# Gated-recurrence keys multiplied by their bound in place, and the diagonal level's products issued with levels 3 and 4

## The chip, the cores and the metric

One core of a Trainium2 chip runs one program. The metric is the device time of one execution in microseconds (us). Engines are named as in the profile: PE (TensorE matmul), PEld (its weight loads), DVE (VectorE), ACT (ScalarE), POOL (GpSimd), SP (SyncE, which here only issues DMAs).

## The reference

Four blocks run one after the other on 256 tokens of width 2048: a gated convolution, the gated recurrence (HGRN2), sliding-window attention, a SwiGLU feed-forward. The change is in the recurrence. Per direction and head (16 heads of 128):

```python
def forget(a, lb):
    log_f = jnp.logaddexp(jnp.log(lb), jnp.log1p(-lb) + jax.nn.log_sigmoid(a))
    key = (1.0 - lb) * jax.nn.sigmoid(-a)
    return heads(log_f), heads(key)
...
        b = jnp.cumsum(fb, axis=2)
...
        decay = jnp.exp(jnp.where(lower_tri, diff, -jnp.inf))
        scores = jnp.einsum("bhtk,bhsk,bhtsk->bhts", qb, kb, decay)
        o_intra = jnp.einsum("bhts,bhsv->bhtv", scores, vb)
```

`lb` is the lower bound of the forget gate. Both directions are added, normalised per head, gated and projected.

## The kernel before

**Weights as the clock of the program.** All weight matrices stream through four slots in chunks of 256 x 512 numbers, 656 of them. For each chunk SP loads `raw`, ACT rounds it to `w_hi` (L889), DVE subtracts to get `w_lo` (L1273; POOL does it in some stretches), and PE issues 12 matmuls of 128 x 512 (L625, L626, L627: w_hi by h_hi, w_lo by h_hi, w_hi by h_lo). ACT may round chunk n once PE has used chunk n-4, DVE waits for ACT, and PE waits for DVE. All other work is hung on this stream: `Hooks` is a table from a tick (the chunk's place in its phase, from 0) to the steps that an engine issues, in program order, right behind its own instruction for that chunk. On PE the steps of tick 8 stand behind the matmuls of chunk 8.

**The recurrence.** The input projection of the recurrence has four iterations of 32 chunks, one for each group j of four heads. The work on group j is issued during the next iteration, and for the last group in the phase that follows (the gate projection). These four stretches, 100 us each from about 470 us on, are called **passes 1 to 4** here (j = 0 to 3), and ticks are counted from 0 to 31 within a pass. Scores are not taken from one product, because the decay between two tokens is a difference of running sums. They are taken in levels: level 1 is the product of the two halves of 128 tokens, levels 2 to 8 are pairs of neighbouring blocks of 64, 32, 16, 8, 4, 2, 1 tokens, and level 0 is the diagonal (a token with itself, no decay). In a pass:

- POOL moves three transposed tiles in blocks of 32 partitions (L503): `kf`, `kb` (the gate inputs of both directions), `qT`, 16 copies each. It is set going by DVE's transposes at tick 28 of the pass before (`quarters`).
- ACT: `gates(0)` at tick 1, `gates(1)` at tick 6 (sigmoids of kf and kb, both signs, behind POOL's moves), `ln_f` for the two directions at 6 and 7, `ln_k` at 8 and 9, `take(0)` at 11, the exponentials of level 1 at 12 and 13, then at 11+2s the exponentials of level s and at 15, 17, 20 `take` of levels 1, 2, 3 (copies out of PSUM).
- DVE: `diagonal` at 6, `scan_f` at 8 and `scan_b` at 9 (running sums), `keys` at 10 and 11, `diffs(2)` at 12, and from 13 on `weigh(s)` at 11+2s and `diffs(s+1)` at 12+2s; `take` of levels 4 to 8 from 21 on.
- PE: level 0 at tick 8, level 1 at 13, level 2 at 14, levels 3 and 4 at 18, 5 and 6 at 22, 7 and 8 at 26, then the products with the values at 26 and 28.

`diagonal` (L1438 on) forms kf x bound + kb x bound into a slot of `E`; `ln_k` takes the logarithm of key x bound, with the bound as ACT's scale, one head at a time, since each head has its own column of bounds. It waits for `diagonal`, since it overwrites the keys. Steps tell each other by counting semaphores: `g_G` (DVE's operands are ready), `g_mm` (PE's level is in PSUM), `g_S` (it has been taken from there). `g_mm` and `g_S` are incremented in the order in which levels are issued.

Of the kernel before, what the change touches and what calls it, by code (L numbers as in the profile page):

```python
# [30 lines left out]
ACT = mybir.ActivationFunctionType  # L31
ALU = mybir.AluOpType
# [4 lines left out]
S = 256  # L37
# [12 lines left out]
HPG = GC // P  # L50
# [114 lines left out]
def build(nc, t, out):  # L165
    ph = phases()
    ctx = ExitStack()
    with ctx:
# [13 lines left out]
        fg = sb(ctx, "fg", [P, TB, GC])  # L182
        ident = sb(ctx, "ident", [P, P])
        feat = sb(ctx, "feat", [P, KT, ROWS])
        eps = sb(ctx, "eps", [P, 2])
# [23 lines left out]
        lbj = sb(mix, "lbj", [P, 2, 2, HPG])  # L209
# [24 lines left out]
        qT = sb(hs, "qT", [P, HPG, S])  # L234
        kf = sb(hs, "kf", [P, HPG, S])
        kb = sb(hs, "kb", [P, HPG, S])
        Bc = sb(hs, "Bc", [P, HPG, S])
        Xc = sb(hs, "Xc", [P, HPG, S])
        E = sb(hs, "E", [P, 2, 2, HPG, S])
        ST = sb(hs, "ST", [P, 2, HPG, 2, P])  # L240
        SB = sb(hs, "SB", [P, HPG, 2, QUARTER])
# [2 lines left out]
        ssh = sb(hs, "ssh", [P, 3, 2 * HPG])  # L244
        powers = sb(hs, "powers", [P, 2 * HPG])
        gate_rows = (aftok, abtok, qtok, sz)
        lf_back = qtok[:, :, :].rearrange("p a (b c) -> p (a b) c", c=S)
        hs.close()

# [26 lines left out]
        T = ctx.enter_context(nc.psum_tensor("T", [P, 4, 512], F32))  # L276
# [2 lines left out]

        def operands(s):  # L280

            b = (s - 1) % 4 if s else 1
            return (E_more if b >= 2 else E)[:, b % 2, :, :, :]

        def gate_banks(k):
            return T01 if k % 2 else T23
# [76 lines left out]
        def flat(ap):  # L363
            return ap.rearrange("p a b -> p (a b)")
# [205 lines left out]
        def _(pe):  # L570
# [138 lines left out]
            at = Hooks().put(4, lambda: v_turn(3))  # L709
# [11 lines left out]
            def level(j, s):  # L721

                pe.wait_ge(g_G, 9 * j + s + 1)
                if s == 0:
                    pe.wait_ge(g_M, 3 * j + 3)
                if s >= 2:
                    pe.wait_ge(g_K, 7 * j + s - 1)
                    pe.wait_ge(g_S, 9 * j + s - 1)
                e = operands(s)
                for h in range(HPG):  # L730
                    for b in range(2):
                        if s == 1:
                            last = nc.tensor.matmul(T[:, h // 2, (h % 2) * S + b * P:(h % 2) * S + b * P + P],  # L733
                                                    e[:, 0, h, b * P:(b + 1) * P], e[:, 1, h, (1 - b) * P:(2 - b) * P],
                                                    start=True, stop=True)
                            continue
                        n = HB if s == 2 else QUARTER
                        for i in range(P // n):
                            at = b * P + i * n
                            to = b * P + (i ^ 1) * n if s in (2, 3) else at  # L740
                            g, q = (e[:, 1, h, at:at + n], qT[:, h, to:to + n]) if s == 0 else (e[:, 0, h, at:at + n], e[:, 1, h, to:to + n])
                            last = nc.tensor.matmul(T[i * n:(i + 1) * n, 2 + s % 2, (2 * h + b) * n:(2 * h + b + 1) * n],  # L742
                                                    g, q, start=True, stop=True)
                last.then_inc(g_mm, 1)

# [10 lines left out]

            def av_across(j):
                pe.wait_ge(g_raw, 4 * j + 4)
                pe.wait_ge(g_S, 9 * j + 2)
                av_products(True)  # L760

            def av(j):
# [2 lines left out]

            def process(j):

                at = Hooks().put(8, lambda: level(j, 0))
                for s in range(1, 9):
                    at.put(13 if s == 1 else 10 + 4 * (s // 2 + s % 2) if s > 2 else 14, lambda s=s: level(j, s))  # L770
                return at.put(26, lambda: av_across(j)).put(28, lambda: av(j))
# [98 lines left out]
        def _(act):  # L870
# [199 lines left out]
            def ln_k(j, d):  # L1070

                act.wait_ge(g_G, 9 * j + 1)
                k = (kf, kb)[d]
                for h in range(HPG):
                    last = A(k[:, h, :], k[:, h, :], ACT.Ln, scale=lbj[:, d, 1, h:h + 1], bias=eps[:, 1:2])
                last.then_inc(g_act, 1)

            def cross_keys(j):

                act.wait_ge(g_D, 15 * j + 1)  # L1080
                for h in range(HPG):
                    A(E[:, 0, 0, h, 0:P], kf[:, h, 0:P], ACT.Exp, bias=Bc[:, h, P - 1:P])
                    A(E[:, 0, 0, h, P:S], kb[:, h, P:S], ACT.Exp, bias=back[:, 1, h:h + 1])

            def cross_queries(j):
                for h in range(HPG):
                    A(E[:, 0, 1, h, 0:P], Xc[:, h, 0:P], ACT.Exp, scale=-1.0, bias=Xc[:, h, P:P + 1])
                    last = A(E[:, 0, 1, h, P:S], Bc[:, h, P:S], ACT.Exp, bias=back[:, 0, h:h + 1])
                last.then_inc(g_E, 1)
# [6 lines left out]

            def take(j, s):

                act.wait_ge(g_mm, 9 * j + s + 1)
                if s == 0:  # L1100
                    A(SB[:, :, :, :].rearrange("p a b c -> p (a b c)"), T[:, 2, 0:S], ACT.Copy).then_inc(g_S, 1)
                    return
                if s == 1:
                    if not is_first(j):
                        act.wait_ge(g_av, j)
                    A(ST[:, 0, :, :, :].rearrange("p a b c -> p (a b c)"), flat(T01), ACT.Copy).then_inc(g_S, 1)
                    return
                c = LEVELS[s - 2]
                ps = T[:, 2 + s % 2, 0:2 * HPG * c].rearrange("p (a c) -> p a c", c=c)
                for i in range(P // c):  # L1110
                    r, o = slice(i * c, (i + 1) * c), (i ^ 1) * c
                    last = A(ST[r, 1, :, :, o:o + c].rearrange("p a b c -> p (a b) c"), ps[r, :, :], ACT.Copy)
                last.then_inc(g_S, 1)
# [15 lines left out]
            def process(j):  # L1129
                at = Hooks().put(1, lambda: gates(j, 0)).put(6, lambda: gates(j, 1))  # L1130
                for d in range(2):
                    at.put(6 + d, lambda d=d: ln_f(j, d)).put(8 + d, lambda d=d: ln_k(j, d))
                at.put(11, lambda: take(j, 0)).put(12, lambda: cross_keys(j)).put(13, lambda: cross_queries(j))
                for s in range(1, 9):
                    if s > 1:
                        at.put(14 if s == 2 else 11 + 2 * s, lambda s=s: exp(j, s))
                    if s < ACT_TAKES:
                        at.put((15, 17, 20)[s - 1], lambda s=s: take(j, s))
                return at.put(29, lambda: blocks(j)).put(31, lambda: o_out(j))
# [112 lines left out]
        def _(dve):  # L1252
# [185 lines left out]
            def diagonal(j):  # L1438

                dve.wait_ge(g_lb, j + 1)  # L1440
                dve.wait_ge(g_act, 6 * j + 2)
                for h in range(HPG):
                    V.tensor_scalar(E[:, 1, 1, h, :], kf[:, h, :], lbj[:, 0, 1, h:h + 1], None, ALU.mult)
                settle()
                for h in range(HPG):
                    last = STT(out=E[:, 1, 1, h, :], in0=kb[:, h, :], scalar=lbj[:, 1, 1, h:h + 1],
                               in1=E[:, 1, 1, h, :], op0=ALU.mult, op1=ALU.add)
                last.then_inc(g_G, 1)

            def scan_f(j):  # L1450

# [38 lines left out]
            def diffs(j, s):  # L1490

                e = operands(s)
                dve.wait_ge(g_mm, 9 * j + max(1, s - 3))
                c = width(s)
                rf, rb = bounds(c)
                fr, bl = halves(Bc[:, :, :], c)[1], halves(Xc[:, :, :], c)[0]
                kl, kr = halves(kf[:, :, :], c)[0], halves(kb[:, :, :], c)[1]
                gl, gr = halves(e[:, 0, :, :], c)
                ql, qr = halves(e[:, 1, :, :], c)
                TT(ql, rb, bl, ALU.subtract)  # L1500
                TT(qr, fr, rf, ALU.subtract).then_inc(g_D, 1)
                TT(gl, rf, kl, ALU.add)
                TT(gr, kr, rb, ALU.subtract).then_inc(g_D, 1)
# [9 lines left out]
            def take(j, s):  # L1513

                settle()
                if s == ACT_TAKES:
                    dve.wait_ge(g_S, 9 * j + s)
                dve.wait_ge(g_mm, 9 * j + s + 1)
                V.memset(none[:, :], 0.0)
                V.copy_predicated(SB[:, :, :, :].rearrange("p a b c -> p (a b) c"),  # L1520
                                  lmask[:, s - ACT_TAKES, :].unsqueeze(1).to_broadcast([P, 8, QUARTER]),
                                  T[:, 2 + s % 2, 0:S].rearrange("p (a c) -> p a c", c=QUARTER)).then_inc(g_S, 1)
# [300 lines left out]
```

## Time and profile before

| | |
|---|---|
| median of 3 runs | 1899.8 us (1899.09 to 1900.17) |
| the profiled execution's own time | 1899.58 us |
| its span | 1897.3 us |
| PE busy | 1891.8 us |
| PEld busy | 1560.9 us |
| DVE busy | 1286.2 us |
| ACT busy | 1057.8 us |
| POOL busy | 614.4 us |
| TensorE clock granted | full in all 40 slices |

How to read it: the span is what the profile covers; 2.3 us of the execution lie around it. Matmuls are recorded as overlapping (a 128 x 512 matmul shows 0.39 us, but the next one starts 0.227 us after it), so PE's busy time says little about its waits: they are read from the distance between the starts of two matmuls. A float32 matmul of the levels leaves two records, so the 32 matmuls of level 0 count as x64 in the trace.

### The profile page before, as it was taken

The page shows a single profiled execution, that of the slowest core. Times are in us where ns is not written, and L with a number is a line of the kernel's source. Part 1 is how long each engine was busy: PE and PEld are TensorE (multiplying, and loading weights), DVE is VectorE, ACT ScalarE, POOL GpSimd, SP SyncE. Part 2 cuts the span into 40 slices and gives each one's busy share as a digit, 9 for nine tenths or more (in the row PEclk, how much of TensorE's full clock was granted, in tenths as well). Part 3 has the DMA queues.
Part 4 walks back from the last instruction along what each step waited for, and adds up shares of the span by engine and source line. Part 5 has one row for each costly group of instructions (what it writes and reads, how often), then busy time and mean ns, then how long its engine had stood idle before and what let it go on. Part 6 is the DMA issues. An engine that isn't in the chain of part 4 may idle for free.

```text
span 1897.3 us, 28818 instructions
## 1 busy us (share of the span) xinstructions
PE 1891.8 (100%) x10864; PEld 1560.9 (82%) x10864; DVE 1286.2 (68%) x1869; ACT 1057.8 (56%) x1402; POOL 614.4 (32%) x641
## 2 busy tenths in 40 slices
PE   9999999999999999999999999999999999999999
PEld 8888878888887888788888888888888888888887
DVE  5899967555888888887668876555555555544443
ACT  7444466456868787875465755444444444443432
POOL 1899852306051423302418641122222222210000
PEclk9999999999999999999999999999999999999999
DMA  9666555666555565555565455666666666655554
GB/s 326 193 190 186 178 171 194 189 195 182 168 176 167 151 185 167 167 161 184 189 190 150 154 174 171 206 191 196 188 191 196 193 194 191 195 193 195 192 195 159
DMA packets 183598, 352.62 MB, mean 186 GB/s; under 512 B 11840, under 2 KB 12352, under 8 KB 183488
## 3 DMA queue, kind: packets, MB, share of 16 engines
q1 hardware_dynamic: 183344, 351.12, 60.1%
q8 instruction: 72, 1.18, 0.3%
q14 instruction: 38, 0.31, 0.0%
q10 hardware_dynamic: 144, 0.01, 0.0%
HBM read 348.99 MB, written 2.10 MB: 185 GB/s over the span
## 4 chain that ended last, share of the span: by engine, by line
PE 88%; DVE 4%; POOL 4%; issue 2%; ACT 2%; DVEq 1%; POOLq 0%; ACTq 0%
PE acc L625 28%; PE acc L627 28%; PE acc L626 28%; POOL kb L503 2%; POOL kf L503 1%; DVE w_lo L1273 1%; PE T L576 1%; DVEq L1259 1%; PE T L742 1%; PE acc L592 1%; PE T L843 0%; ACT w_hi L889 0%; PE T L733 0%; DVE Xc L1461 0%; PE T L822 0%
## 5 line engine op out<-in xcount | busy, mean ns | idle before, releaser
L1273 DVE TENSOR_TENSOR w_lo<-raw,w_hi 128x1024 fp32r<-128x1024 f32 x564 | 694.9, 1235 | 518.1 <-ACT w_hi L889 508.6
L889 ACT ACTIVATE w_hi<-raw 128x1024 fp32r<-128x1024 f32 x655 | 687.5, 1058 | 609.7 <-PE acc L627 589.4
L625 PE MATMUL acc<-w_hi,h_hi 128*128 128x512 f32 x1872 | 736.0, 393 | 1.0 <-DVE w_lo L1273 0.9
L627 PE MATMUL acc<-w_hi,h_lo 128*128 128x512 f32 x1872 | 729.5, 390 | 0.0
L626 PE MATMUL acc<-w_lo,h_hi 128*128 128x512 f32 x1872 | 729.4, 390 | 0.0
L625 PEld LDWEIGHTS acc<-w_hi,h_hi 128*128 128x128 f32 x1872 | 351.7, 188 | 79.9 <-issue 4.5
L627 PEld LDWEIGHTS acc<-w_hi,h_lo 128*128 128x128 f32 x1872 | 351.6, 188 | 73.5
L626 PEld LDWEIGHTS acc<-w_lo,h_hi 128*128 128x128 f32 x1872 | 351.8, 188 | 70.7
L565 POOL COPY fT<-fq 32x256 f32<-32x256 f32 x176 | 110.8, 630 | 398.9 <-DVE fq L1755 392.0
L474 POOL TENSOR_TENSOR w_lo<-raw,w_hi 128x1024 fp32r<-128x1024 f32 x80 | 190.4, 2407 | 68.1 <-ACT w_hi L889 67.9
L1364 DVE SCALAR_TENSOR_TENSOR T<-vpad,feat,T 128x256 f32<-128x256 f32 x464 | 182.5, 493 | 0.0
L625 PE MATMUL acc<-w_hi,y_hi 128*128 128x512 f32 x384 | 151.3, 394 | 0.0
L626 PE MATMUL acc<-w_lo,y_hi 128*128 128x512 f32 x384 | 149.7, 390 | 0.0
L627 PE MATMUL acc<-w_hi,f_lo 128*128 128x512 f32 x352 | 137.1, 389 | 0.0
L625 PE MATMUL acc<-w_hi,f_hi 128*128 128x512 f32 x352 | 137.1, 389 | 0.0
L626 PE MATMUL acc<-w_lo,f_hi 128*128 128x512 f32 x352 | 137.1, 389 | 0.0
L503 POOL COPY kf<-sz 32x256 f32<-32x256 f32 x64 | 37.3, 582 | 279.1 <-DVEq L1259 276.6
L627 PE MATMUL acc<-w_hi,hy_lo 128*128 128x512 f32 x256 | 99.8, 390 | 0.0
L625 PEld LDWEIGHTS acc<-w_hi,y_hi 128*128 128x128 f32 x384 | 72.1, 188 | 17.3 <-DVE y_lo L1278 1.5
L626 PEld LDWEIGHTS acc<-w_lo,y_hi 128*128 128x128 f32 x384 | 72.2, 188 | 14.5
L625 PEld LDWEIGHTS acc<-w_hi,f_hi 128*128 128x128 f32 x352 | 66.1, 188 | 13.7
L626 PEld LDWEIGHTS acc<-w_lo,f_hi 128*128 128x128 f32 x352 | 66.1, 188 | 13.7
(254 smaller groups left out, 1556.2 us busy)
## 6 DMA issues: line engine op xcount, KB each, us to landing
raw<-in_hgrn_w_in_dram SPq DMA_DIRECT2D x160, 512.0 KB, 3.6
raw<-in_conv_w_in_dram SPq DMA_DIRECT2D x96, 512.0 KB, 4.2
raw<-in_ffn_w_gate_dram SPq DMA_DIRECT2D x88, 512.0 KB, 4.3
raw<-in_ffn_w_up_dram SPq DMA_DIRECT2D x88, 512.0 KB, 3.8
raw<-in_ffn_w_down_dram SPq DMA_DIRECT2D x88, 512.0 KB, 4.4
raw<-in_attn_w_qkv_dram SPq DMA_DIRECT2D x40, 512.0 KB, 3.7
raw<-in_conv_w_out_dram SPq DMA_DIRECT2D x32, 512.0 KB, 4.2
raw<-in_hgrn_w_out_dram SPq DMA_DIRECT2D x32, 512.0 KB, 4.0
```

The source lines that it names most:

```text
L474: nc.gpsimd.tensor_tensor(w_lo[:, slot, :, :], raw[:, slot, :, :], rounded(w_hi[:, slot, :, :]), ALU.subtract).then_inc(split_ready, 1)
L503: last = nc.gpsimd.tensor_copy(turned_block(dst, a, b), own_block(src, a, b))
L565: last = nc.gpsimd.tensor_copy(turned_block(fT, a, b), own_block(fq, a, b))
L576: last = nc.tensor.transpose(dst[:, q // 2, at:at + P], src[:, tb, q * P:(q + 1) * P], ident[:, :])
L592: last = nc.tensor.matmul(acc[:, 0, tb, :], stationary[:, n * CK + kk, a], moving[:, n, kk, :], start=first and kk == 0, stop=False)
L625: nc.tensor.matmul(o, hi[:, kt, a], w_hi[:, slot, kk, :], start=c == 0 and kk == 0, stop=False)
L626: nc.tensor.matmul(o, hi[:, kt, a], w_lo[:, slot, kk, :], start=False, stop=False)
L627: last = nc.tensor.matmul(o, lo[:, kt, a], w_hi[:, slot, kk, :], start=False, stop=c == p.chunks - 1 and kk == CK - 1)
L742: last = nc.tensor.matmul(T[i * n:(i + 1) * n, 2 + s % 2, (2 * h + b) * n:(2 * h + b + 1) * n], g, q, start=True, stop=True)
L889: A(w_hi[:, slot, :, :], raw[:, slot, :, :], ACT.Copy).then_inc(hi_ready, 1)
L1273: TT(w_lo[:, slot, :, :], raw[:, slot, :, :], rounded(w_hi[:, slot, :, :]), ALU.subtract).then_inc(split_ready, 1)
L1364: STT(out=cy[:, kt, :] if tap == TAPS - 1 else y, in0=v, scalar=w, in1=y, op0=ALU.mult, op1=ALU.add).then_inc(c_tap, 1)
```

## The change

1. `diagonal` (DVE): both key tiles are multiplied by their bound in place, four instructions of one head for each direction; then one addition of the two tiles into `same`, which is the memory of `fg` (a tile not in use in these passes). Before, four multiplications wrote into `E` and four multiply-adds finished the sum.
2. `ln_k` (ACT): the scale is gone, so one logarithm of 128 x 1024 stands for four of 128 x 256, in each direction.
3. Level 0 moves on PE from tick 8 to tick 18, ahead of level 3, and writes to PSUM bank 0 instead of 2. Its `take` moves on ACT from tick 11 to 20, ahead of level 3's. `place(s)` gives the new position in the counts of `g_mm` and `g_S`, and the waits follow it.

```diff
+        same = fg[:, :, :].rearrange("p a (b c) -> p (a b) c", c=S)
...
+            b = (s - 1) % 4
...
+        def place(s):
+            return {1: 1, 2: 2, 0: 3}.get(s, s + 1)
...
                 if s == 0:
                     pe.wait_ge(g_M, 3 * j + 3)
+                    pe.wait_ge(g_S, 9 * j + place(1))
                 if s >= 2:
                     pe.wait_ge(g_K, 7 * j + s - 1)
-                    pe.wait_ge(g_S, 9 * j + s - 1)
+                    if s > 4:
+                        pe.wait_ge(g_S, 9 * j + place(s - 2))
+                    elif s > 2:
+                        pe.wait_ge(g_S, 9 * j + place(2))
+                    elif j:
+                        pe.wait_ge(g_S, 9 * j)
...
-                at = Hooks().put(8, lambda: level(j, 0))
+                at = Hooks().put(18, lambda: level(j, 0))
...
                 act.wait_ge(g_G, 9 * j + 1)
-                k = (kf, kb)[d]
-                for h in range(HPG):
-                    last = A(k[:, h, :], k[:, h, :], ACT.Ln, scale=lbj[:, d, 1, h:h + 1], bias=eps[:, 1:2])
-                last.then_inc(g_act, 1)
+                k = flat((kf, kb)[d][:, :, :])
+                A(k, k, ACT.Ln, bias=eps[:, 1:2]).then_inc(g_act, 1)
...
-                act.wait_ge(g_mm, 9 * j + s + 1)
+                act.wait_ge(g_mm, 9 * j + place(s))
...
-                at.put(11, lambda: take(j, 0)).put(12, lambda: cross_keys(j)).put(13, lambda: cross_queries(j))
+                at.put(20, lambda: take(j, 0)).put(12, lambda: cross_keys(j)).put(13, lambda: cross_queries(j))
...
-                for h in range(HPG):
-                    V.tensor_scalar(E[:, 1, 1, h, :], kf[:, h, :], lbj[:, 0, 1, h:h + 1], None, ALU.mult)
+                for d, k in enumerate((kf, kb)):
+                    for h in range(HPG):
+                        V.tensor_scalar(k[:, h, :], k[:, h, :], lbj[:, d, 1, h:h + 1], None, ALU.mult)
                 settle()
-                for h in range(HPG):
-                    last = STT(out=E[:, 1, 1, h, :], in0=kb[:, h, :], scalar=lbj[:, 1, 1, h:h + 1],
-                               in1=E[:, 1, 1, h, :], op0=ALU.mult, op1=ALU.add)
-                last.then_inc(g_G, 1)
+                TT(same, kf[:, :, :], kb[:, :, :], ALU.add).then_inc(g_G, 1)
...
             def diffs(j, s):
                 e = operands(s)
-                dve.wait_ge(g_mm, 9 * j + max(1, s - 3))
+                if s > 4:
+                    dve.wait_ge(g_mm, 9 * j + place(s - 4))
```

PE at tick 18 of pass 1, before (the 64 matmuls are levels 3 and 4, 32 each):

```order
L627 MATMUL acc<-w_hi,h_lo 128x512
L742 MATMUL T<-E_more 32x32 x64
L625 MATMUL acc<-w_hi,h_hi 128x512
```

and with the change, where the lines are numbered anew:

```order
L632 MATMUL acc<-w_hi,h_lo 128x512
L753 MATMUL T<-qT,fg 32x32 x32
L753 MATMUL T<-E_more 32x32 x64
L630 MATMUL acc<-w_hi,h_hi 128x512
```

The 32 matmuls of level 0 now stand in front of the other two levels at tick 18; at tick 8 the chunks follow one another.

DVE from tick 6 to tick 8 of pass 2, before:

```order
L1443 TENSOR_SCALAR E<-kf,lbj 128x256 x4
L1446 SCALAR_TENSOR_TENSOR E<-kb,lbj,E 128x256 x4
L1272 REGISTER_ALU
L1273 TENSOR_TENSOR w_lo<-raw,w_hi 128x1024
L1272 REGISTER_ALU
L1273 TENSOR_TENSOR w_lo<-raw,w_hi 128x1024
L1452 REGISTER_ALU
L1454 SCALAR_TENSOR_TENSOR Bc<-Bc 128x256 x4
```

and with the change:

```order
L1453 TENSOR_SCALAR kf<-kf,lbj 128x256 x4
L1453 TENSOR_SCALAR kb<-kb,lbj 128x256 x4
L1455 TENSOR_TENSOR fg<-kf,kb 128x1024
L1281 REGISTER_ALU
L1282 TENSOR_TENSOR w_lo<-raw,w_hi 128x1024
L1281 REGISTER_ALU
L1282 TENSOR_TENSOR w_lo<-raw,w_hi 128x1024
L1459 REGISTER_ALU
L1461 SCALAR_TENSOR_TENSOR Bc<-Bc 128x256 x4
```

The eight instructions ahead of chunk 7's w_lo have become nine; behind it nothing has moved up to the scan (the last row of each, four heads).

ACT at ticks 20 and 21 of pass 1 with the change:

```order
L900 ACTIVATE w_hi<-raw 128x1024
L1108 REGISTER_ALU
L1110 ACTIVATE SB<-T 128x256
L1108 REGISTER_ALU
L1121 ACTIVATE ST<-T 32x8x32 x4
L899 REGISTER_ALU
L900 ACTIVATE w_hi<-raw 128x1024
```

`SB<-T` is level 0's take, which was at tick 11; it now stands between chunk 20's w_hi and level 3's take (the x4 row), ahead of chunk 21's w_hi.

## Rows read from the trace of the kernel before

**Rows 1.** The page: the span, and PE's busy time.

```profile
span 1897.3 us, 28818 instructions
...
PE 1891.8 (100%) x10864; PEld 1560.9 (82%) x10864; DVE 1286.2 (68%) x1869; ACT 1057.8 (56%) x1402; POOL 614.4 (32%) x641
```

**Rows 2.** Timeline, PE, tick 8 of pass 1 (start us, duration us, engine, line, op).

```profile
481.02 0.39 PE L626 MATMUL acc<-w_lo,h_hi 128*128 128x512 f32 x1
481.25 0.39 PE L627 MATMUL acc<-w_hi,h_lo 128*128 128x512 f32 x1
481.57 0.76 PE L742 MATMUL T<-qT,E 128*32 128x32 f32 x64
...
482.60 0.40 PE L626 MATMUL acc<-w_lo,h_hi 128*128 128x512 f32 x1
```

**Rows 3.** Timeline, PE, tick 18 of pass 2: levels 3 and 4.

```profile
613.15 0.39 PE L627 MATMUL acc<-w_hi,h_lo 128*128 128x512 f32 x1
613.47 1.41 PE L742 MATMUL T<-E_more 128*32 128x32 f32 x128
...
615.15 0.40 PE L626 MATMUL acc<-w_lo,h_hi 128*128 128x512 f32 x1
```

**Rows 4.** Timeline, DVE: w_lo of chunk 13, passes 1 to 4.

```profile
491.30 1.22 DVE L1273 TENSOR_TENSOR w_lo<-raw,w_hi 128x1024 fp32r<-128x1024 f32 x1
...
592.51 1.22 DVE L1273 TENSOR_TENSOR w_lo<-raw,w_hi 128x1024 fp32r<-128x1024 f32 x1
...
692.35 1.22 DVE L1273 TENSOR_TENSOR w_lo<-raw,w_hi 128x1024 fp32r<-128x1024 f32 x1
...
793.05 1.22 DVE L1273 TENSOR_TENSOR w_lo<-raw,w_hi 128x1024 fp32r<-128x1024 f32 x1
```

**Rows 5.** Timeline, PE: first matmul of chunk 13 (585.25: of chunk 10), passes 1 to 4.

```profile
493.30 0.39 PE L625 MATMUL acc<-w_hi,h_hi 128*128 128x512 f32 x1
...
585.25 0.50 PE L625 MATMUL acc<-w_hi,h_hi 128*128 128x512 f32 x1 [0.48 <-DVE w_lo L1273]
...
593.78 0.51 PE L625 MATMUL acc<-w_hi,h_hi 128*128 128x512 f32 x1
594.12 0.40 PE L626 MATMUL acc<-w_lo,h_hi 128*128 128x512 f32 x1
...
693.63 0.50 PE L625 MATMUL acc<-w_hi,h_hi 128*128 128x512 f32 x1
...
794.32 0.50 PE L625 MATMUL acc<-w_hi,h_hi 128*128 128x512 f32 x1
```

**Rows 6.** Timeline, DVE, ticks 6 to 10 of pass 2: diagonal, w_lo of chunks 7, 8, 10.

```profile
569.51 1.64 DVE L1443 TENSOR_SCALAR E<-kf,lbj 128x256 f32<-128x256 f32 x4 [2.42 <-ACT kb L1059]
571.23 2.09 DVE L1446 SCALAR_TENSOR_TENSOR E<-kb,lbj,E 128x256 f32<-128x256 f32 x4
573.86 1.23 DVE L1273 TENSOR_TENSOR w_lo<-raw,w_hi 128x1024 fp32r<-128x1024 f32 x1 [0.54 <-ACT w_hi L889]
576.78 1.22 DVE L1273 TENSOR_TENSOR w_lo<-raw,w_hi 128x1024 fp32r<-128x1024 f32 x1 [1.69 <-ACT w_hi L889]
...
583.97 1.23 DVE L1273 TENSOR_TENSOR w_lo<-raw,w_hi 128x1024 fp32r<-128x1024 f32 x1 [0.15 <-issue]
```

**Rows 7.** Timeline, ACT, ticks 6 to 8 of pass 2: gates(1), chunk 8's w_hi, ln_k.

```profile
567.47 1.06 ACT L1058 ACTIVATE qtok<-kb 128x1024 f32<-128x1024 f32 x1 [1.63 <-POOL kb L503]
...
575.70 1.04 ACT L889 ACTIVATE w_hi<-raw 128x1024 fp32r<-128x1024 f32 x1
576.65 2.07 ACT L1075 ACTIVATE kf<-kf,eps,lbj 128x256 f32<-128x256 f32 x4
```

**Rows 8.** Timeline, POOL: the moves of qT in pass 2.

```profile
567.42 8.38 POOL L503 COPY qT<-abtok 32x256 f32<-32x256 f32 x16
```

**Rows 9.** Timeline, ACT tick 20 of pass 2, and POOL at pass 2's end.

```profile
614.27 1.54 ACT L1112 ACTIVATE ST<-T 32x256 f32<-32x256 f32 x4 [1.90 <-PE T L742]
...
641.18 9.74 POOL L503 COPY kf<-sz 32x256 f32<-32x256 f32 x16 [65.39 <-DVEq L1259]
```

More of the change, by code:

```diff
@@ L280, in operands @@
         def operands(s):
-            b = (s - 1) % 4 if s else 1
+            b = (s - 1) % 4
             return (E_more if b >= 2 else E)[:, b % 2, :, :, :]
+        def place(s):
+            return {1: 1, 2: 2, 0: 3}.get(s, s + 1)
         def gate_banks(k):
@@ L740, in level @@
                             to = b * P + (i ^ 1) * n if s in (2, 3) else at
-                            g, q = (e[:, 1, h, at:at + n], qT[:, h, to:to + n]) if s == 0 else (e[:, 0, h, at:at + n], e[:, 1, h, to:to + n])
-                            last = nc.tensor.matmul(T[i * n:(i + 1) * n, 2 + s % 2, (2 * h + b) * n:(2 * h + b + 1) * n],
+                            g, q = (same[:, h, at:at + n], qT[:, h, to:to + n]) if s == 0 else (e[:, 0, h, at:at + n], e[:, 1, h, to:to + n])
+                            last = nc.tensor.matmul(T[i * n:(i + 1) * n, 2 + s % 2 if s else 0, (2 * h + b) * n:(2 * h + b + 1) * n],
                                                     g, q, start=True, stop=True)
@@ L758, in av_across @@
                 pe.wait_ge(g_raw, 4 * j + 4)
-                pe.wait_ge(g_S, 9 * j + 2)
+                pe.wait_ge(g_S, 9 * j + place(0))
                 av_products(True)
@@ L1097, in take @@
             def take(j, s):
-                act.wait_ge(g_mm, 9 * j + s + 1)
+                act.wait_ge(g_mm, 9 * j + place(s))
                 if s == 0:
-                    A(SB[:, :, :, :].rearrange("p a b c -> p (a b c)"), T[:, 2, 0:S], ACT.Copy).then_inc(g_S, 1)
+                    A(SB[:, :, :, :].rearrange("p a b c -> p (a b c)"), T[:, 0, 0:S], ACT.Copy).then_inc(g_S, 1)
                     return
@@ L1516, in take @@
                 if s == ACT_TAKES:
-                    dve.wait_ge(g_S, 9 * j + s)
-                dve.wait_ge(g_mm, 9 * j + s + 1)
+                    dve.wait_ge(g_S, 9 * j + place(s - 1))
+                dve.wait_ge(g_mm, 9 * j + place(s))
                 V.memset(none[:, :], 0.0)
```

## The prediction

> **What bounds the kernel now.** First the page: PE is busy for 1891.8 of 1897.3 us [rows 1]. That figure only says that matmul records touch each other; whether PE ever waits is read from the starts. Two neighbouring 128 x 512 matmuls start 0.23 us apart (481.02, 481.25 [rows 2]), so a chunk of twelve takes 2.72 us, and 656 chunks take 1784 us of the 1897. What is left are the small matmuls and the waits. So a change in the recurrence can move the time in two ways only: by PE's own small matmuls, or by making chunks late.
>
> Second, the timeline of PE against the one of DVE, chunk by chunk, in passes 1 to 4. Nearly everywhere a chunk's w_lo is ready well before PE wants it. The exception is ticks 7 to 13. There ACT and DVE carry the logarithms, the scans and the first differences, and w_lo comes just in time. Chunk 10 of pass 2 starts at 585.25 after 0.48 us idle, named to DVE [rows 5]; its w_lo ran from 583.97 to 585.20 [rows 6]. Chunk 13 of pass 2: w_lo from 592.51 [rows 4], so done at 593.73, and PE's first matmul at 593.78 [rows 5]. Pass 3: done 693.57, start 693.63. Pass 4: done 794.27, start 794.32. In these three passes PE starts chunk 13 0.05 us after DVE delivers. In pass 1 it does not: done 492.52, start 493.30, so 0.78 us of slack.
>
> Third, the chain of waits, to see what sets w_lo of chunk 13. Backwards in pass 2: DVE runs without a pause worth the name from chunk 8's w_lo (576.78) over both scans, keys and differences to 592.51. Chunk 8's w_lo began when ACT had finished chunk 8's w_hi (575.70 + 1.04), after 1.69 us of waiting [rows 6, 7]. ACT came there through gates(1), a table load and both ln_f, and gates(1) began at 567.47, when POOL had moved kb, after 1.63 us of waiting [rows 7]. POOL's moves are set going by DVE's transposes at tick 28 of the pass before, as in pass 3 at 641.18 [rows 9]. And between tick 18 and 28 that chain hangs on PE: ACT's take(3) at 614.27 had waited 1.90 us for PE's level 3 [rows 9], chunk 21's w_hi stands behind it, chunk 21's w_lo behind that, and from there DVE and ACT hand on to each other up to tick 28. So the loop is: PE tick 18, ACT, DVE, POOL, ACT, DVE, PE chunk 13, PE tick 18.
>
> **PE: level 0 moves.** At tick 8, from the last matmul before the group (481.25) to the second after it (482.60) are 1.35 us; two plain steps of 0.227 would be 0.45. So the group costs 0.90 us [rows 2]. At tick 18 the same distance is 615.15 - 613.15 = 2.00, less 0.45: 1.55 us for two levels [rows 3]. With a fixed part f and u per level, f + u = 0.90 and f + 2u = 1.55: u = 0.65, f = 0.25. So 0.90 goes from tick 8, 0.65 is added at tick 18. If PE were the only limit the change would gain 0.25 us a pass, 1.0 us in all.
>
> But the 0.90 lies ahead of chunk 13. In passes 2 to 4 PE would only wait for DVE longer: chunk 13 starts when its w_lo is done, and this chain does not pass through level 0. **Gain there: nothing.** In pass 1 chunk 13 can start earlier until it meets w_lo: 493.30 - 492.57 = 0.73 us, less the slower second step behind a wait (594.12 - 593.78 = 0.34 in place of 0.227, so 0.11 [rows 5]). **Gain: 0.6 us.** The 0.65 us lies behind chunk 13 and ahead of level 3, since level 0 is issued first. In pass 1 it goes through take(3), w_hi of chunk 21 and tick 28 to POOL and so to chunk 13 of pass 2; likewise from 2 to 3 and 3 to 4; in pass 4 nothing waits behind it, and it is plain PE time. **Loss: 4 x 0.65 = 2.6 us.** Sum: +2.0 us.
>
> **DVE: diagonal.** Before: four multiplications, a drain and the first multiply-add's start take 571.23 - 569.51 = 1.72 us, 0.43 each, and the multiply-adds 2.09 [rows 6]. Now: 8 x 0.43 = 3.44 and one addition of 128 x 1024, priced by the w_lo subtraction of the same size, 1.23: 4.67, from 569.51 to 574.2 in place of 573.3. Bounds: not below the 3.8 of before (eight instructions of the cheaper kind plus an addition do more than eight did); above, each of the nine waits for one of POOL's copies, 8.38 / 16 = 0.52 us each [rows 8]: 8 x 0.52 + 0.52 + 1.23 = 5.9, until 575.4. I take 4.67, as its parts are rows of the very stretch. Behind it stands chunk 7's w_lo (573.86 before, so 0.3 us late, 1.5 at the upper bound), then chunk 8's, which waits for ACT until 576.78. The diagonal may thus end at 576.78 - 1.23 = 575.55 before chunk 8's w_lo moves. Even the upper bound stays under it. Chunk 7's matmuls may start up to a microsecond late; PE has 0.90 us less to do before chunk 10 and waits there 0.48 us already, so this too is swallowed. **Cost: 0.** The cover is ACT's ln_f; were it gone, each microsecond would count in every pass.
>
> Here the Trainium skill speaks against the change: SBUF — State Buffer, section "Who interferes with whom", says that a VectorE instruction in a two-port mode (tensor_scalar in float32 can be one) or with two SBUF inputs, and a GpSimd instruction, take a shared port pair as an exclusive lock, so that the later one blocks fully. The trace agrees in kind, as DVE's 0.43 us steps lie beside POOL's copies of 0.52. By the rule the change puts five more lock-takers into the stretch, and the upper bound above would hold: the same sum, since 575.4 is still in time.
>
> **ACT: ln_k.** Four logarithms of a head take 2.07 us; one of 128 x 1024 should take 1.04, like the w_hi row beside it [rows 7]. Two directions: 2 us less on ACT per pass. It stands behind chunk 8's w_hi, so it can bring forward only the w_hi of chunks 9 to 12. None of these is what DVE waits for: its scans and keys come between. The logarithm also waits for the diagonal, done by 574.2 (at most 575.4), ahead of its own start at 576.65. **Gain: 0.** take(0) at tick 20 runs while PE does level 3, in the 1.90 us for which ACT waits there [rows 9]. **Cost: 0.** POOL's qT has until weigh(1) at tick 13. The wait of diffs(2) for level 0 falls away; it had long been met. SP's loads keep their order.
>
> **Sum.** The profiled execution took 1899.58 us, the median is 1899.8. +2.0 gives 1901.6 to 1901.8; I say 1901.7. A measurement of this kernel tells about 0.2% (3.8 us) from no change, so this counts as no change.
>
> **The rivals.**
> (a) *PE's own count.* The waits at chunks 10 and 13 shrink with PE's work and only the instruction count is left: -1.0 us, 1898.8. For it: pass 1 has slack. Against: the 0.05 us between w_lo and matmul in three passes. 12%.
> (b) *The added 0.65 us does not go round the loop*, for instance because ACT or DVE, not PE, is last somewhere between tick 18 and 28: then +0.65 in pass 4 alone, -0.6 in pass 1, about 1899.9. 13%.
> (c) *ACT's 2 us reach the chain* and all waits of ticks 7 to 13 go. The largest one seen is the 0.48 us at chunk 10 [rows 5]; two of that size and some tenths at chunks 7 to 9 make 1.1 us a pass, an estimate from that row, 3.4 in passes 2 to 4, so with (a) -4.4, 1895.4. Against: DVE's row, not ACT's, ends last at chunks 10 and 13. 3%.
> (d) *The diagonal becomes the bound, slower.* Place: DVE between 569.5 and chunk 8's w_lo. It decides once the eight multiplications and the addition take more than 6.0 us, or (6.0 - 1.23) / 8 = 0.60 us per multiplication. If each waited for two of POOL's copies (1.04 us), diagonal = 8.3 + 1.2 + 0.5 = 10 us, 4 us over, at chunk 13 of each pass: 2.0 + 4 x 4 = 1918. If it is 0.1 us over 0.60 each: 0.8 x 4 = 3.2 more, 1904.9. 6%.
> (e) *Some small extra per pass* (a level that is now just late at tick 22 or 26, 0.2 to 0.5 us): 1902.6 to 1903.8. 8%.
> My own forecast, 1901.0 to 1902.6, has 58%.
>
> **Range and chances.** From (a)'s 1898.8, the lowest case that has weight, to 1903.4 in the middle of (e). Faster by over 0.2% (under 1896.0) is (c) alone: 0.03. Slower (over 1903.6) is (d) and an end of (e): 0.09. The rest, 0.88, is no change.
>
> **What would show it.** Right: small matmuls only at ticks 13, 14, 18, 22, 26, 28; the group at tick 18 lasting 0.65 us longer; PE's first matmul of chunk 13 0.05 us behind w_lo in all four passes, the wait for DVE ahead of chunk 10 about 1.4 us in pass 2; passes about 0.65 us longer from chunk 13 to chunk 13. Wrong: chunk 8's w_lo right behind the diagonal without a wait for ACT would be (d); chunk 13 with slack in passes 2 to 4 would be (a) or (c); POOL's first kf copy at the same distance from tick 18's start as before would be (b).

## The result and the profile after

The changed kernel takes 1907.03 us (median of 6 runs, 1904.17 to 1907.26), the one before beside it 1899.34 us (6 runs, 1897.71 to 1900.17): ratio 1.0035, 95% interval 1.0025 to 1.0045. It is slower, by 7.7 us between the medians (their own ratio is 1.0040), where 2.0 us were predicted: the 1901.7 us, with 1903.4 as the upper end, were wrong. The profiled execution is one of 1907.26 us, with a span of 1905.0.

The page of the changed kernel, span, busy times and the queue that brings instructions (packets, MB, share of 16 engines):

```profile
span 1905.0 us, 28796 instructions
...
PE 1894.3 (99%) x10864; PEld 1561.0 (82%) x10864; DVE 1291.5 (68%) x1873; ACT 1051.0 (55%) x1378; POOL 616.9 (32%) x641
...
q8 instruction: 72, 1.18, 0.3%
```

The span grew by 7.7 us, PE's busy time by only 2.5 [rows 1]. What PE waited for (us in total, times, longest), first before, then after the change:

```profile
PE T L583 <- POOL ones L462: 1.1, 1, 1.1
PE acc L625 <- DVE w_lo L1273: 0.9, 2, 0.5
```

```profile
PE acc L630 <- DVE w_lo L1282: 2.9, 5, 0.7
PE acc L631 <- issue: 2.7, 1, 2.7
PE T L588 <- POOL ones L467: 1.1, 1, 1.1
```

Two things are new. The waits for DVE are 2.0 us more, in kind what the prediction meant by "PE would only wait for DVE longer"; the one ahead of chunk 10 in pass 2, named there as a sign, grew from 0.48 to 0.72 us and not to 1.4. The other row is one wait of 2.7 us for "issue", that is, for nothing that the profile shows. PE's timeline at tick 18 of pass 4 has it:

```profile
815.80 0.39 PE L632 MATMUL acc<-w_hi,h_lo 128*128 128x512 f32 x1
816.12 0.76 PE L753 MATMUL T<-qT,fg 128*32 128x32 f32 x64
816.73 1.35 PE L753 MATMUL T<-E_more 128*32 128x32 f32 x128
818.02 0.50 PE L630 MATMUL acc<-w_hi,h_hi 128*128 128x512 f32 x1
818.35 0.39 PE L631 MATMUL acc<-w_lo,h_hi 128*128 128x512 f32 x1
818.58 0.40 PE L632 MATMUL acc<-w_hi,h_lo 128*128 128x512 f32 x1
818.82 0.39 PE L630 MATMUL acc<-w_hi,h_hi 128*128 128x512 f32 x1
821.93 0.79 PE L631 MATMUL acc<-w_lo,h_hi 128*128 128x512 f32 x1 [2.72 <-issue]
822.52 0.63 PE L632 MATMUL acc<-w_hi,h_lo 128*128 128x512 f32 x1
822.94 0.63 PE L630 MATMUL acc<-w_hi,h_hi 128*128 128x512 f32 x1
...
825.46 0.40 PE L630 MATMUL acc<-w_hi,h_hi 128*128 128x512 f32 x1
```

The joined group is over, chunk 19 has begun, its w_lo has long been there, and after four matmuls PE stands still: 3.11 us from start to start in place of 0.23. Behind the stop the steps are 0.43 us instead of 0.23. In the kernel before, the same four matmuls of chunk 19 and the fifth behind them follow one another without a stop:

```profile
814.00 1.36 PE L742 MATMUL T<-E_more 128*32 128x32 f32 x128
815.29 0.50 PE L625 MATMUL acc<-w_hi,h_hi 128*128 128x512 f32 x1
...
816.09 0.39 PE L625 MATMUL acc<-w_hi,h_hi 128*128 128x512 f32 x1
816.32 0.39 PE L626 MATMUL acc<-w_lo,h_hi 128*128 128x512 f32 x1
```

With the change, the windows are (us, busy of PE, PEld, DVE, ACT, POOL, granted clock, DMA share, GB/s):

```profile
815.00:820.00 5.00, 4.21 (x202) 3.18 (x200) 3.80 (x6) 2.83 (x7) 0.00 (x0) 1.00 0.73 213
820.00:825.00 5.00, 3.07 (x7) 2.50 (x8) 4.63 (x7) 2.99 (x4) 0.00 (x0) 0.70 0.40 110
825.00:830.00 5.00, 5.00 (x22) 4.09 (x21) 4.50 (x6) 3.91 (x4) 0.00 (x0) 0.96 0.50 130
```

TensorE's granted clock, at its full 2.4 GHz until the stop, was then at 1.2 GHz for about 3.4 us. That made the rest of chunk 19 1.7 us longer.

**Where the 7.7 us are.** Chunk 13 of passes 1 to 4 starts at:

```profile
492.77 0.50 PE L630 MATMUL acc<-w_hi,h_hi 128*128 128x512 f32 x1
...
593.37 0.50 PE L630 MATMUL acc<-w_hi,h_hi 128*128 128x512 f32 x1
...
695.11 0.50 PE L630 MATMUL acc<-w_hi,h_hi 128*128 128x512 f32 x1
...
796.47 0.50 PE L630 MATMUL acc<-w_hi,h_hi 128*128 128x512 f32 x1
```

In pass 4 it is 796.47 - 794.32 = 2.15 later than before [rows 5], of which 0.2 was there already at the first chunk of the recurrence's input projection, ahead of pass 1 (369.26 against 369.07). The rest, to the last matmul, is 1104.42 us against 1099.13, so 5.3 more: 0.65 for the added level, 2.9 for the stop, 1.7 for the half clock. Sum 0.2 + 1.95 + 0.65 + 2.9 + 1.7 = 7.4; the other 0.3 lies behind the last matmul.

The stretch of the diagonal, DVE in pass 2 after the change:

```profile
568.90 1.64 DVE L1453 TENSOR_SCALAR kf<-kf,lbj 128x256 f32<-128x256 f32 x4 [1.08 <-ACT kb L1070]
570.46 1.83 DVE L1453 TENSOR_SCALAR kb<-kb,lbj 128x256 f32<-128x256 f32 x4
572.37 1.29 DVE L1455 TENSOR_TENSOR fg<-kf,kb 128x1024 f32<-128x1024 f32 x1
573.58 1.41 DVE L1282 TENSOR_TENSOR w_lo<-raw,w_hi 128x1024 fp32r<-128x1024 f32 x1
576.16 1.23 DVE L1282 TENSOR_TENSOR w_lo<-raw,w_hi 128x1024 fp32r<-128x1024 f32 x1 [1.18 <-ACT w_hi L900]
```

It took 573.66 - 568.90 = 4.76 us (4.67 predicted), and chunk 8's w_lo (576.16) still waits for ACT. ACT's logarithms, 2.07 us before [rows 7], take 1.14:

```profile
576.04 1.14 ACT L1085 ACTIVATE kf<-kf,eps 128x1024 f32<-128x1024 f32 x1
```

### The profile page after: what moved, and what is told of

It is laid out like the page before. It is cut to its first block, busy times and chain, and to the rows that moved or that the text cites. A ratio compares the mean times of both kernels' runs of the same rounds, so it can differ in the third digit from the quotient of the medians.

```text
span 1905.0 us, 28796 instructions
## 1 busy us (share of the span) xinstructions
PE 1894.3 (99%) x10864; PEld 1561.0 (82%) x10864; DVE 1291.5 (68%) x1873; ACT 1051.0 (55%) x1378; POOL 616.9 (32%) x641
## 4 chain that ended last, share of the span: by engine, by line
PE 88%; DVE 4%; POOL 4%; issue 2%; ACT 1%; DVEq 1%; POOLq 0%; ACTq 0%
PE acc L630 28%; PE acc L632 28%; PE acc L631 28%; POOL kb L508 2%; DVE w_lo L1282 1%; POOL kf L508 1%; PE T L581 1%; PE T L753 1%; DVEq L1268 1%; PE acc L597 1%; ACT w_hi L900 0%; PE T L854 0%; PE T L744 0%; DVE Xc L1468 0%; PE T L833 0%
## 5 line engine op out<-in xcount | busy, mean ns | idle before, releaser
L632 PEld LDWEIGHTS acc<-w_hi,f_lo 128*128 128x128 f32 x352 | 66.1, 188 | 13.8
```

Source lines behind the costliest of these rows:

```text
L632: last = nc.tensor.matmul(o, lo[:, kt, a], w_hi[:, slot, kk, :], start=False, stop=c == p.chunks - 1 and kk == CK - 1)
```

## The experiments

Theory A: the move of level 0 makes PE's small matmuls one burst of 96, and in it, or just behind, PE runs out of instructions where a boundary of its instruction stream falls; the rest is the predicted loop. Theory B: the keys and the diagonal delay the passes, and the stop has to do with them or with chance.

**One part alone.** `e1_keys_only` keeps the keys, the diagonal and the single logarithms, and puts level 0 back (its PSUM bank and its waits too):

```diff
-                at = Hooks().put(18, lambda: level(j, 0))
+                at = Hooks().put(8, lambda: level(j, 0))
...
-                at.put(20, lambda: take(j, 0)).put(12, lambda: cross_keys(j)).put(13, lambda: cross_queries(j))
+                at.put(11, lambda: take(j, 0)).put(12, lambda: cross_keys(j)).put(13, lambda: cross_queries(j))
```

> The change without its move: keys multiplied in place, one addition, one logarithm per direction, but level 0 at tick 8 again (bank 2, take at tick 11). Theory A (all the added time hangs on tick 18: 0.65 us per pass round the loop, and one stop of PE of 1.5 to 4.6 us behind the longer burst of small matmuls, because its instructions are loaded too late): within 0.6 us of the kernel before, no stop of PE inside a chunk. Theory B (the diagonal on DVE, in contention with POOL, lengthens the chain of passes 2 and 3): 2 us or more above the kernel before, with chunk 7's or chunk 8's w_lo later against POOL's end.

1899.54 us against 1898.86, ratio 1.0005 (0.9996 to 1.0014), and no wait for issue. The medians lie 0.7 us apart, just over the 0.6 expected and not to be told from nothing. The three periods from chunk 13 to chunk 13 add up to 301.05 us (before 301.02).

`e2_level_only` is the other half: level 0 at tick 18, with the old diagonal and logarithms.

```diff
-                for d, k in enumerate((kf, kb)):
-                    for h in range(HPG):
-                        V.tensor_scalar(k[:, h, :], k[:, h, :], lbj[:, d, 1, h:h + 1], None, ALU.mult)
+                for h in range(HPG):
+                    V.tensor_scalar(same[:, h, :], kf[:, h, :], lbj[:, 0, 1, h:h + 1], None, ALU.mult)
...
-                TT(same, kf[:, :, :], kb[:, :, :], ALU.add).then_inc(g_G, 1)
+                for h in range(HPG):
+                    last = STT(out=same[:, h, :], in0=kb[:, h, :], scalar=lbj[:, 1, 1, h:h + 1],
+                               in1=same[:, h, :], op0=ALU.mult, op1=ALU.add)
+                last.then_inc(g_G, 1)
```

> The move alone: level 0 with levels 3 and 4 at tick 18, the diagonal with its four multiplications and four multiply-adds (into the new tile), four logarithms per direction. Theory A: as the changed kernel, 4.8 to 7.7 us above the kernel before, with the stop of PE in pass 4, since PE's instructions are the same ones in the same places. Theory B: at most 3 us above the kernel before.

1905.33 us, ratio 1.0033 (1.0021 to 1.0044), 6.5 us above the kernel before, inside the expected 4.8 to 7.7: the move has nearly the whole loss. The stop is at the same place in pass 4, PE's timeline:

```profile
818.08 0.40 PE L630 MATMUL acc<-w_hi,h_hi 128*128 128x512 f32 x1
821.13 0.50 PE L631 MATMUL acc<-w_lo,h_hi 128*128 128x512 f32 x1 [2.66 <-issue]
821.47 0.40 PE L632 MATMUL acc<-w_hi,h_lo 128*128 128x512 f32 x1
```

In this execution the steps behind it are plain: granted clock 1.00 in each window, span 1902.3. So the move alone brings the stop, and the half clock may or may not follow it. Its periods add up to 302.57, 1.55 more than before; from there to the end it takes 1102.73, 3.6 more than before, 0.65 + 2.9.

**The position of the instructions.** Counting PE's records from the first (weight loads, matmuls and what its queue holds besides), the stop lies at record 10689 in both traces. If it is a matter of position, instructions added far ahead must shift it in the program. `e3_shift64` adds 64 instructions before the first chunk. They take 1.1 us there (6.46 to 7.59), and the recurrence's first chunk starts 0.9 us later than with the change (370.16 for 369.26):

```diff
+            for i in range(16):
+                nc.tensor.matmul(T[0:QUARTER, 0, 0:QUARTER], ones[:, 0:QUARTER], ones[:, 0:QUARTER], start=True, stop=True)
```

> The changed kernel with 16 tiny extra matmuls (64 instructions in PE's queue, about 0.3 us) behind the warm-up, at the very start. All that follows is the same work, but lies 64 instructions later in the 256-instruction loads of PE's code. Theory A: the stop of PE at chunk 19 of pass 4 goes or comes at another burst; if it goes, about 3 us above the kernel before. If the stop has nothing to do with the loads of code: still at chunk 19 of pass 4, time as the changed kernel, 4.8 to 7.7 us above the kernel before.

1911.83 us, ratio 1.0069 (1.0055 to 1.0083), 13.0 us above the kernel before: neither outcome that was expected. Now there are two stops, in passes 3 and 4, both inside the burst. Waits, then timeline:

```profile
PE T L755 <- issue: 6.0, 2, 3.2
```

```profile
715.17 1.31 PE L755 MATMUL T<-E_more 128*32 128x32 f32 x122
719.66 0.33 PE L755 MATMUL T<-E_more 128*32 128x32 f32 x6 [3.19 <-issue]
...
820.86 1.11 PE L755 MATMUL T<-E_more 128*32 128x32 f32 x100
824.77 0.64 PE L755 MATMUL T<-E_more 128*32 128x32 f32 x28 [2.79 <-issue]
```

They lie at records 8897 and 10689, which are 7 x 256 apart. The granted clock was at half for 6.8 us from 718.83 on and for 3.4 us from 824.64 on. Of the 4.8 us above the changed kernel the added work has 0.9; the second stop (3.2 us) and the longer half clock are more than enough for the rest. The stop of pass 4 kept its place in the instruction stream, while the work standing there changed; the one of pass 3 is new. `e5_shift192` adds 192 instructions in the same way (48 matmuls, 3.2 us).

> The changed kernel with 48 tiny extra matmuls (192 instructions in PE's queue, about 0.5 us) behind the warm-up. All four stops seen so far lie at a place in PE's instruction stream that leaves the same remainder when divided by 256 (193, counted from the first record), and only where the load before it falls due early in the burst of tick 18. By that rule (Theory A) the stop of pass 4 goes, and stops of about 3 us appear in passes 1 and 2, each with 1.7 us of half clock or without: 8 to 13 us above the kernel before. If the stops belong to a place in the work and not in the instruction stream: a stop in pass 4 and none in pass 1.

1908.51 us, ratio 1.0046 (1.0031 to 1.0061), 8.9 us above the kernel before, inside the expected 8 to 13; 2.3 of them are there already at the recurrence's first chunk. The stops are in passes 1 and 2 now, as expected, and none in pass 4; the second is shorter than expected, and the half clock (3.4 us) followed only the first:

```profile
515.39 1.16 PE L755 MATMUL T<-E_more 128*32 128x32 f32 x103
519.34 0.47 PE L755 MATMUL T<-E_more 128*32 128x32 f32 x25 [2.79 <-issue]
...
620.19 0.93 PE L755 MATMUL T<-E_more 128*32 128x32 f32 x81
622.54 0.62 PE L755 MATMUL T<-E_more 128*32 128x32 f32 x47 [1.42 <-issue]
```

**The length of the burst.** `e4_tick16` is the changed kernel with level 0 alone at tick 16, so that no burst is longer than before:

```diff
-                at = Hooks().put(18, lambda: level(j, 0))
+                at = Hooks().put(16, lambda: level(j, 0))
```

> The changed kernel with level 0 issued at tick 16 by itself, its take still at tick 20, so no burst is longer than in the kernel before. It costs 0.90 us in place of 0.65 in each pass, still ahead of level 3. Theory A: no stop of PE, 1 us more than the changed kernel without its stop: 3.0 to 4.0 us above the kernel before. If the stop has another cause: 5.8 to 8.7 us above it.

1903.49 us, ratio 1.0022 (1.0013 to 1.0032), and no stop. PE's timeline at tick 18 of pass 4, and its waits:

```profile
817.40 0.39 PE L632 MATMUL acc<-w_hi,h_lo 128*128 128x512 f32 x1
817.72 1.36 PE L753 MATMUL T<-E_more 128*32 128x32 f32 x128
819.01 0.51 PE L630 MATMUL acc<-w_hi,h_hi 128*128 128x512 f32 x1
```

```profile
PE acc L630 <- DVE w_lo L1282: 2.7, 5, 0.7
```

The stop is gone and the loop is left. The median is 4.6 us above the kernel before, between the two outcomes that were expected (3.0 to 4.0, 5.8 to 8.7). In the profiled execution chunk 13 of pass 1 starts 0.7 us earlier than before, the three periods add 304.58 - 301.02 = 3.6 us and the rest 0.9: 3.8 us. The prediction's own sum, with 0.90 for a group by itself, gives 4 x 0.90 - 0.6 = 3.0.

**The loop.** In `e6_level0_last` the joined group has the order 3, 4, 0, and level 0's take stands behind level 3's, so the 0.65 us lie behind what ACT waits for.

```diff
-                at = Hooks().put(18, lambda: level(j, 0))
+                at = Hooks()
...
+                at.put(18, lambda: level(j, 0))
```

> The changed kernel with level 0 behind levels 3 and 4 at tick 18, and its take behind level 3's at tick 20. The same instructions on PE, so Theory A still has the stop in pass 4 (2.9 us, or 4.6 us with half clock). Level 3 is no longer delayed, so by the loop (tick 18, ACT, DVE, POOL, ACT, DVE, chunk 13) the three periods from chunk 13 to chunk 13 are 0.65 us shorter each than with the change, 2 us in all: 3.0 to 4.7 us above the kernel before. If the loop does not hang on level 3: as the changed kernel, 4.8 to 7.7 us above it.

1905.52 us, ratio 1.0031 (1.0019 to 1.0044). The three periods add up to 300.99, 2.7 less than after the change (303.70) and like before. So the 0.65 does go round by way of level 3, rival (b) is out, and one can take it off that way by order alone. The stop stayed (2.69 us, PE goes on at 818.98). The total is 5.95 us above the kernel before and not the 3.0 to 4.7 expected. In the profiled execution (1905.84) the clock was at half for 6.8 us, from 818.15 on, still in the stop, which costs 3.0 us in place of 1.7; the other five runs, at mean clocks of 0.999 and 1.000, took 1904.4 to 1906.8, so this is not the whole of it:

```profile
815.00:820.00 5.00, 2.31 (x25) 1.55 (x13) 3.42 (x6) 4.69 (x7) 0.00 (x0) 0.81 0.40 118
820.00:825.00 5.00, 5.00 (x13) 3.94 (x12) 4.89 (x7) 2.14 (x3) 0.00 (x0) 0.50 0.60 193
```

**Towards a better version.** The loop's narrow place is ticks 7 to 13, where DVE waits for ACT's w_hi behind ln_f. `e7_logs_later` is `e1_keys_only` with ACT's `ln_f` of the backward direction and both `ln_k` one tick later:

```diff
-                    at.put(6 + d, lambda d=d: ln_f(j, d)).put(8 + d, lambda d=d: ln_k(j, d))
+                    at.put((6, 8)[d], lambda d=d: ln_f(j, d)).put(9 + d, lambda d=d: ln_k(j, d))
```

> The keys' part of the change alone (level 0 at tick 8), and ACT's ln_f of the backward direction moved from tick 7 to 8, ln_k to 9 and 10, so that chunk 8's w_hi comes 2 us sooner. If the chain to chunk 13 runs through ACT's work ahead of chunk 8's w_hi and then DVE's program order, it is 1.5 to 2 us shorter and the waits of PE in ticks 7 to 13 of passes 2 to 4 go: 2.0 to 3.4 us under the kernel before. If DVE alone sets chunks 10 and 13: no change.

1898.33 us against 1899.57, ratio 0.9994 (0.9985 to 1.0003): less than expected. Chunk 13 has slack again (2.03, 0.20, 0.21, 0.35 us in the four passes), but PE now waits at chunk 7, which stands behind the longer diagonal:

```profile
575.57 0.50 PE L630 MATMUL acc<-w_hi,h_hi 128*128 128x512 f32 x1 [0.34 <-DVE w_lo L1276]
```

`e8_level0_with1` joins level 0 to level 1 at tick 13 instead of its own tick 8, a burst of 64, on top of that:

```diff
-                at = Hooks().put(8, lambda: level(j, 0))
+                at = Hooks()
...
+                at.put(13, lambda: level(j, 0))
```

> As e7_logs_later, and level 0 behind level 1 at tick 13 (bank 3, its take behind level 1's at tick 15), where the burst is short. If PE no longer waits in ticks 7 to 13, joining saves the 0.25 us fixed part in each pass: 3.0 to 4.4 us under the kernel before, no stop of PE. If the loop still binds: level 0 lies ahead of level 3 again and costs 0.65 in each pass, so about as the kernel before or 2 us above it.

1900.57 us, ratio 1.0006 (0.9997 to 1.0015), no stop, and chunk 13 is again 0.06 us behind its w_lo in passes 2 to 4. The expectation for the case that the loop still binds (up to 2 us above the kernel before) is the one that came true. The two kernels stand 2.2 us apart: joining gains nothing here, since work taken from ahead of chunk 13 is work put behind it, and chunk 13 has no slack any more.

`e9_logs_old_keys` is the kernel before with only that one line of ACT's order changed; `e10_split` is `e7_logs_later` where the forward multiplications no longer wait for the backward direction.

> The kernel before with nothing changed but ACT's order: ln_f of the backward direction at tick 8, ln_k at 9 and 10 (four logarithms of a head each, as before). If ACT's 2 us per pass that the new keys save matter once chunk 8's w_hi is early, this is slower than e7_logs_later by about 1 us in each of passes 2 to 4; if not, it is the same or, with its shorter diagonal (3.8 us for 4.6 measured), faster by 0.3 us per pass. Against the kernel before: 0 to 3 us less.

> As e7_logs_later, but DVE multiplies the forward keys as soon as gates(0) is done and waits for gates(1) only ahead of the backward keys. In e7_logs_later DVE stood idle ahead of the diagonal, and chunk 7's w_lo came 0.5 us late behind it. With four of the eight multiplications (1.7 us) out of the way that wait goes: 0.3 to 0.6 us less per pass than e7_logs_later, 2 to 3.5 us under the kernel before. If chunk 7's wait only moves to chunks 10 and 13: as e7_logs_later, 1.2 us under it.

```diff
-                dve.wait_ge(g_act, 6 * j + 2)
                 for d, k in enumerate((kf, kb)):
+                    dve.wait_ge(g_act, 6 * j + 1 + d)
```

`e10_split`: 1897.73 us against 1899.42, ratio 0.9991 (0.9982 to 1.0000), 1.7 us less, where 2 to 3.5 were expected if chunk 7's wait went and 1.2 if it only moved. The wait at chunk 7 is gone from the list of PE's waits. `e9_logs_old_keys`: 1896.82 us (11 runs, 1896.26 to 1897.16), ratio 0.9986 (0.9977 to 0.9995). It is the fastest of all, ahead of both kernels of this case, by 2.6 us of the one before, inside the expected 0 to 3. The list of waits shows nothing that holds PE up any more in the recurrence (the one row left is at the start of the kernel):

```profile
span 1894.6 us, 28818 instructions
```

```profile
PE T L583 <- POOL ones L462: 1.1, 1, 1.1
```

Chunk 13 has 1.96, 1.16, 0.10 and 0.87 us of slack. Between `e9_logs_old_keys` and `e7_logs_later` lie 1.5 us (1.4, each against the kernel before beside it), which is what the keys of the change cost once ACT no longer covers the longer diagonal.

## Why the prediction was wrong, point by point

**"PE: level 0 moves": the failing step.** It took the joined group as PE time alone, "with a fixed part f and u per level", and put the bringing of its instructions at nothing without asking for it. As time for the records its price holds: behind the group PE was 0.65 us later in each pass. The burst is 384 records in 1.8 us, 5 ns each, where a chunk has 24 in 2.72 us, 113 ns each. The instruction queue q8 brings 16 KB packets, in passes 1 to 4 about one for every 256 of PE's records (26 over 27 such stretches), and between 818.9 and 821.9 us, the stop, it brought one:

```profile
q8 instruction: 1, 0.02, 2.0%
```

All seven stops lie at record numbers that leave 193 when divided by 256, in the burst of tick 18 or 8 records behind it, and only where the number 256 lower lay in the same burst. The traces have the queue's packets one by one, and in all seven the packet came only after PE had passed that lower number, and PE went on 1.2 to 1.5 us after it had landed (times in us):

| kernel, pass | record | PE passes the record 256 lower | packet | PE starts the record |
|---|---|---|---|---|
| changed, 4 | 10689 | 816.76 | 819.64 to 820.58 | 821.93, stop |
| `e2_level_only`, 4 | 10689 | 816.02 | 818.77 to 819.69 | 821.13, stop |
| `e6_level0_last`, 4 | 10689 | 813.84 | 816.68 to 817.61 | 818.98, stop |
| `e3_shift64`, 3 | 8897 | 715.06 | 717.38 to 718.34 | 719.66, stop |
| `e3_shift64`, 4 | 10689 | 820.57 | 821.62 to 823.27 | 824.76, stop |
| `e5_shift192`, 1 | 5313 | 515.13 | 516.92 to 517.79 | 519.34, stop |
| `e5_shift192`, 2 | 7105 | 619.73 | 620.35 to 621.31 | 622.54, stop |
| before, 4 | 10689 | 814.03 | 811.66 to 812.69 | 816.10, none |
| changed, 1 | 5057 | 512.51 | 510.88 to 511.86 | 513.74, none |

The last two rows show that two such places close together are not enough. In pass 1 of the changed kernel both lie in the burst, 1.2 us apart, and there is no stop: the packet had landed before the first. There the first place is the 17th record of the burst (in pass 4 of the kernel before the 9th); in the seven stops it is between the 36th and the 138th. In passes 2 and 3 only one such place lies in the burst. A burst of 256 records (levels 3 and 4 before, or `e4_tick16`) never stopped. So the length of the burst and its place in the instruction stream are shown to make the stop, and PE waiting for a packet of q8 fits all nine rows. Why the packet comes late is not shown: in the 2.88 us before the one of 819.64 the queue of the weights, q1, was busy for 0.7 of the 16 DMA engines, and no run took the weight loads away from there. Price: 2.9 us in one pass of four, and 1.7 more where the clock falls behind it. Without these 4.6 us the changed kernel would stand at about 1902.4, inside the range. None of the rivals had the stop; range and chances held no place for a new kind of wait on PE itself.

The Trainium skill, Runtime: NRT & Kernel Launch, section "Instruction fetch mechanics", says that an engine's instruction memory is refilled in 16 KiB blocks of 256 instructions and that the cost of crossing a boundary is "mostly hidden". The trace agrees with the blocks (16 KB packets, multiples of 256 records between stops) and not with the second part where small matmuls are joined: 2.7 to 3.2 us for a crossing, once 1.4.

**The loop: right in kind, and right in size as far as single executions tell.** Chunk 13 is 0.05 us behind w_lo in all four passes, pass 1 too, where the slack of 0.78 was used up as predicted, and `e6_level0_last` shows that the path goes by level 3. The sum was to be 2.0 us. Without the stop, and counted from the recurrence's first chunk, it is 1.95 + 0.65 = 2.6 in the changed kernel and 1.5 in `e2_level_only`, which has the same order on PE (-0.7 up to chunk 13 of pass 1, +1.55, +0.65); in `e4_tick16` it is 3.8, where the sum with its 0.90 per group is 3.0. Single periods scatter by up to 1.9 us between kernels (from pass 2 to 3: 99.85 before, 101.74 after), so the size can be read from sums only, and to about 1 us. That `e4_tick16` loses 0.9 more than the changed kernel in the three periods (3.6 against 2.7) is nearly its dearer group, 3 x 0.25 = 0.75.

**Diagonal, 4.67 us and cost 0: right.** 4.76 us, done at 573.66 with chunk 8's w_lo still waiting for ACT until 576.16, and `e1_keys_only` is within 0.05% of the kernel before. The step also named its cover, ACT's ln_f: with that gone, in `e7_logs_later` against `e9_logs_old_keys`, the keys cost 1.5 us. The multiplications stayed near 0.43 us each and the upper bound of 5.9 was not reached, but not because nothing blocked. In pass 2 each of the last six multiplications starts some 0.03 us after one of POOL's copies and ends 0.15 us after that copy has ended, one for one, 0.44 us apart. The copy that begins beside the addition takes 1.30 us (572.62 to 573.91), where the copies just before it take 0.39 to 0.40. This agrees with the full blocking that the Trainium skill states (SBUF — State Buffer, "Who interferes with whom"). The mechanism of the upper bound was thus at work, and its price of 0.52 was the mean of all 16 copies, the blocked ones among them. By the same rule of the Trainium skill the change puts one lock-taker more into the stretch and not five, since the four multiply-adds that it replaces had two inputs in SBUF each. Rival (d) is out.

**ln_k, gain 0: right.** 2 us fewer on ACT each pass moved nothing in `e1_keys_only`. Rival (c) had a sound idea in the wrong place: taking the waits of ticks 7 to 13 away is worth 2.6 us, but it takes ACT's order, not a shorter ln_k.

**Rival (a)**, PE's own count, would have needed slack at chunk 13: out. **(e)**, "some small extra per pass", with 1902.6 to 1903.8, has `e4_tick16` (1903.49) in its range; of the stop it knew nothing.

**The two groups of times.** The changed kernel's six runs are 1904.2 and 1904.5, and four of 1906.8 to 1907.3. The lower two have a mean granted clock of 1.000, the other four, the profiled 1907.26 among them, of 0.998 or 0.999; 3.4 us at half clock in 1905 make 0.9991. So the lower two are runs without a stretch of half clock behind the stop, as in the trace of `e2_level_only`. The groups are 2.7 us apart and the half clock costs 1.7 in the trace; the other 1.0 is open.

## What to carry to other kernels

Joining groups of tiny instructions is not free even where each alone was: look at how many instructions come in how few microseconds, and keep bursts as short as those that the kernel is seen to live with. Work moved from ahead of a point where an engine waits to behind it is lost twice, since the wait takes up the gain and the loop takes the added time. Where a loop of waits sets the pace, the order of a short stretch on the engine that feeds it (here one line of ACT's) is worth more than fewer instructions there.

## What the runs showed of the hardware

- PE can stop for 2.7 to 3.2 us (once 1.4) with all its inputs there, at fixed positions of its instruction stream, every time at a multiple of 256 records from each other; the profile calls it "issue". It goes on 1.2 to 1.5 us after a 16 KB packet of the instruction queue has landed. 64 tiny matmul instructions at the very start, 1.1 us of work, changed which work stands at these positions, and the time by 4.8 us (1911.83 against 1907.03).
- A stop of 2.7 to 3.2 us can be followed by TensorE at 1.2 GHz, for 3.4 us in the changed kernel, 6.8 us in `e6_level0_last` (granted clock 0.50, from 0.8 us before PE went on) and 6.8 and 3.4 us in `e3_shift64`, and was not in `e2_level_only`. In the profiled execution of the changed kernel that is a third of what was lost behind chunk 13.
- In the changed kernel a multiplication of 128 x 256 on DVE beside POOL's copies takes the pace of the copies, 0.44 us each, and a copy that begins beside an addition of 128 x 1024 with two inputs takes 1.30 us in place of 0.40.
